# A float32 decoder trunk on one core: one activation table for the roots, memory turns inside the last values' projection, late weights turned a pass apart

## The reference

```python
mem_n = rmsnorm(mem, mem_norm_g)
y = rmsnorm(x, mix_norm_g) @ w_in              # q, k, v, gates of three head groups
fo = rmsnorm(forgetting_attention(q, k, v, log_f))   # 8 heads of 64
ho = rmsnorm(hgrn2_recurrence(hq, hf, hi)) * silu(hg) # 4 heads of 64
co = silu(channel_group_norm(causal_depthwise_conv(cu * sigmoid(cg), conv_w)))
x = x + concat([fo, ho, co]) @ w_out
# cross attention: q from x, k and v from the memory
k, v = split(mem_n @ w_xkv)
x = x + softmax(q @ k.T / 16) @ v @ w_xo
# mixture of 16 gated experts, top 1 group of 4, top 2 experts in it
x = x + sum_over_chosen(combine * (silu(t @ w_gate) * (t @ w_up)) @ w_down)
return rmsnorm(x, final_norm_g)
```

## Time and profile before

| What | us |
|---|---|
| median of 3 runs | 714.07 (713.83 to 714.19) |
| the profiled execution, its own time | 712.32 |
| its span | 710.3 |
| TensorE busy | 681.3 (96%) |
| VectorE busy | 280.6 (40%) |
| ScalarE busy | 153.2 (22%) |
| GpSimd busy | 78.5 (11%) |
| weight loads of TensorE | 331.4 (47%) |

### The profile page before, as it was taken

One profiled execution on the slowest core, in us unless ns is written; L12 is line 12 of the kernel. 1 busy time (PEld: TensorE's weight loads), 2 busy tenths in 40 slices (PEclk: granted clock), 3 DMA queues, 4 the chain that ended last, 5 costly groups with the idle time before them and its releaser, 6 DMA issues.

```text
span 710.3 us, 8420 instructions
## 1 busy us (share of the span) xinstructions
PE 681.3 (96%) x3398; PEld 331.4 (47%) x3398; DVE 280.6 (40%) x669; ACT 153.2 (22%) x315; POOL 78.5 (11%) x106
## 2 busy tenths in 40 slices
PE   7999999999999999999999999999999999999993
PEld 4644445453547665444444446545565333333331
DVE  3107599927034665213220006513334821212156
ACT  3011351003273444211000104301211010101112
POOL 3000081402020000000000000000001011110062
PEclk9999999999999999999999999999999999999998
DMA  8803240303036513300019406030029999999763
GB/s 288 308 0 119 82 154 1 119 1 108 15 119 180 178 60 119 118 1 0 1 36 395 161 0 237 0 119 30 30 87 341 363 372 389 376 375 392 268 219 137
DMA packets 69939, 111.90 MB, mean 158 GB/s; under 512 B 5648, under 2 KB 43780, under 8 KB 69900
## 3 DMA queue, kind: packets, MB, share of 16 engines
q1 hardware_dynamic: 65724, 96.16, 39.1%
q0 software_dynamic: 4176, 15.21, 5.8%
HBM read 101.90 MB, written 9.46 MB: 157 GB/s over the span
## 4 chain that ended last, share of the span: by engine, by line
PE 87%; DMA 4%; DVE 3%; ACT 3%; issue 1%; POOL 1%; SPq 0%; DVEq 0%; POOLq 0%; ACTq 0%
PE bank L1917 26%; PE bank L2193 16%; PE bank L1792 11%; PE bank L1927 6%; PE bank L1821 5%; PE bank L2263 2%; PE bank L1963 2%; PE bank L2243 2%; PE bank L2146 2%; PE bank L1949 2%; DMA W<-y_dram,A 2%; PE bank L1774 1%; PE bank L2124 1%; PE bank L2133 1%; PE bank L2035 1%; DMA x_sb<-in_x_dram 1%
## 5 line engine op out<-in xcount | busy, mean ns | idle before, releaser
L1917 PE MATMUL bank<-hT,W 128*128 128x512 f32 x368 | 159.7, 593 | 0.9 <-DVE hT L1071 0.9
L2193 PE MATMUL bank<-W,n_sb 128*128 128x512 f32 x256 | 114.2, 596 | 0.7 <-ACT n_sb L1039 0.7
L1917 PEld LDWEIGHTS bank<-hT,W 128*128 128x128 f32 x368 | 69.4, 190 | 87.5 <-issue 86.0
L1792 PE MATMUL bank<-W,A 128*32 128x512 f32 x672 | 84.8, 594 | 1.5 <-DVE A L1162 1.5
L2193 PEld LDWEIGHTS bank<-W,n_sb 128*128 128x128 f32 x256 | 47.1, 190 | 53.9 <-issue 52.3
L1425 DVE SCALAR_TENSOR_TENSOR A<-A,pc 128x511 f32<-128x511 f32 (+29 forms) x60 | 51.6, 860 | 2.0
L695 POOL TENSOR_TENSOR rstd<-ss,mhalf 128x1 f32<-128x1 f32 x14 | 7.7, 550 | 367.6 <-DVE ss L1055 203.1
L1792 PEld LDWEIGHTS bank<-W,A 128*32 128x32 f32 x672 | 23.1, 110 | 49.6 <-issue 47.6
L1821 PE MATMUL bank<-Dn,A 128*32 128x512 f32 x264 | 36.3, 595 | 0.0
L906 ACT ACTIVATE A<-bank 128x512 f32<-128x512 f32 (+1 forms) x22 | 12.1, 556 | 103.7 <-PE bank L1917 77.0
L1277 DVE TENSOR_TENSOR A<-A,bank 128x256 f32<-128x256 f32 x12 | 5.1, 421 | 71.7 <-ACT A L825 71.7
(11 more groups left out here) (306 smaller groups left out, 818.5 us busy)
## 6 DMA issues: line engine op xcount, KB each, us to landing
W<-in_w_gate_dram SPq DMA_DIRECT2D x14, 1024.0 KB, 13.3
W<-in_w_up_dram SPq DMA_DIRECT2D x14, 1024.0 KB, 14.5
Dn<-in_w_down_dram SPq DMA_DIRECT2D x11, 1024.0 KB, 13.8
W<-in_w_in_dram SPq DMA_DIRECT2D x5, 2048.0 KB, 9.3
W<-in_w_xkv_dram SPq DMA_DIRECT2D x4, 2048.0 KB, 8.3
hT<-in_w_down_dram SPq DMA_DIRECT2D x5, 1024.0 KB, 12.7
y_dram<-A POOLq DMA_DIRECT2D x10, 512.0 KB, 7.1
W<-in_w_out_dram SPq DMA_DIRECT2D x2, 2048.0 KB, 8.0
```

The source lines that it names most:

```text
L1792: mm = nc.tensor.matmul(PS[2 + b][r, :], xgT[:, b, c, r], gu_at[GU_HOME[e]][:, c, :], start=c == 0, stop=c == DC - 1)
L1917: mm = nc.tensor.matmul(bank[0:w, 0:n], lhs, src[:, c, 0:n], start=c == 0, stop=c == DC - 1)
L2193: mm = nc.tensor.matmul(PS[k % 4][:, :], src[:, c, t * P:(t + 1) * P], W[:, (n_load + n) % SLOTS, c, :], start=first and j == 0, stop=last ...
```

## The change

Three edits. On ScalarE, the table with Ln and Exp is asked for ahead of the convolution's roots. On TensorE, the last values' group (26) is written out as `last_values`, and the two halves of the memory's tile 1 are turned ahead of its chunks 4 and 6; on VectorE the two copies of tile 0 stand ahead of the heads' scalings, those of tile 1 behind. In the experts, the two late turns stand at the ends of passes 2 and 4 and their copies in passes 3 and 5.

```diff
--- before.py
+++ after.py
@@ -944,6 +944,7 @@
             ho_evac(0)
             proj_evac(22, 23)
             act.wait_ge(consts, 2)
+            nc.scalar.preload_act_table_set("natural_log_exp_and_others")
             for c in range(2):
                 act.wait_ge(cvar, c + 1)
                 inv_root(c, PS[4 + c][:, :], croot[c], crs)
@@ -1293,8 +1294,8 @@
                     y_half(p - 1)
                 if p == 1:
                     late_rows()
-                if 3 <= p < 3 + LATE:
-                    late_turned(p - 3)
+                if p in (3, 5):
+                    late_turned(p // 2 - 1)
 
             def add_row(k, t, w):
                 dve.wait_ge(fin_in[t][k], 16)
@@ -1529,6 +1530,8 @@
 
             for t in range(MT):
                 normed(dve, 1, t, mem_sb, mem_sb)
+            for k in range(2):
+                turn_evac(dve, 1, 0, k, PS[6 + k], memT, R_MEM)
             for p in range(HP):
                 dve.wait_ge(ho_rs, p + 1)
                 nc.vector.scalar_tensor_tensor(out=hob[p], in0=hob[p], scalar=pc[:, R_HG + p:R_HG + p + 1],
@@ -1536,8 +1539,8 @@
                 dve.wait_ge(ho_step, 2 * p + 1)
                 nc.vector.tensor_tensor(catT[:, 4 + p], hob[p], hgT[:, p], ALU.mult).then_inc(ho_step, 1)
 
-            for k in range(2 * MT):
-                turn_evac(dve, 1, k // 2, k % 2, PS[6 + k % 2], memT, R_MEM)
+            for k in range(2):
+                turn_evac(dve, 1, 1, k, PS[6 + k], memT, R_MEM)
 
 
             def f_scores(u, a):
@@ -1860,8 +1863,8 @@
 
                     pe.wait_ge(ht_sb, p)
                 turn_hidden(p % 2, ht_ps)
-                if 2 <= p < 2 + LATE:
-                    turn_late(p - 2)
+                if p in (2, 4):
+                    turn_late(p // 2 - 1)
             down_pass(NP - 1)
 
             pe.wait_ge(over_done, 1)
@@ -2108,10 +2111,16 @@
             pe.wait_ge(ho_sb, HP)
             for k in range(2):
                 turn_group(pe, 1, 0, k, PS[6 + k], mem_sb)
-            g = run([along(1, 3, 0, FW)], g, 5)
-            for k in range(2):
-                pe.wait_ge(turn_sb, TURN0[1] + k + 1)
-                turn_group(pe, 1, 1, k, PS[6 + k], mem_sb)
+            def last_values(bank):
+                for c in range(DC):
+                    if c in (4, 6):
+                        k = c // 2 - 2
+                        pe.wait_ge(turn_sb, TURN0[1] + k + 1)
+                        turn_group(pe, 1, 1, k, PS[6 + k], mem_sb)
+                    mm = nc.tensor.matmul(bank[:, 0:FW], hT[:, c, 3 * P:4 * P], W[:, 1, c, 0:FW], start=c == 0, stop=c == DC - 1)
+                return mm
+
+            g = run([last_values], g, 5)
 
 
             def qk(u):
```

## The result

The changed kernel took 708.40 us, the median of 5 executions (707.64 to 710.46). The kernel before, run beside it on the same chip, took 713.83 (5 executions, 712.83 to 714.19).

What follows compares the result with a forecast made beforehand. TensorE was taken as the bound (87% of the chain), so time is won where it stands still. Memory's gap 2.75 + late weights 1.05 = 3.8 us, subtracted from the median 714.07, gave 710.3 us, range 709.5 to 711.6.

Steps and rivals of the forecast that it cites:

- The memory's gap: Before the memory's first key projection on TensorE: it starts at 211.85 in place of 214.60, a gain of 2.75 us.
- The rival in which the table doesn't shorten the roots: ScalarE's roots stay slow: 1.35 + 1.05 = 2.4 us gained, 711.7 us in all; chance 0.06.
- The fallback of 1.35: Memory's gap if the roots stay slow: key projection at 213.25, so 1.35 us gained instead of 2.75.
- The four loads at the convolution's roots: Four of ScalarE's removed table loads, at the convolution: priced at nothing, covered by the values projections on TensorE.
- The mask of the second pair: VectorE's mask reading the second pair's decay sums: 4.0 us of room, 3.63 taken, 0.4 left; priced at nothing.
- The late weights: Turns of late tables in the expert passes: 1.31 us gained on TensorE, 1.05 counted after a wait at pass 10.
- pass 10 waits about 0.2: With TensorE 1.31 us earlier, pass 10 waits about 0.2 for up weights that had a margin of 1.11.
- bounds from 0 to 1.31: Late edit's gain: 1.31 us if the weights slip in, 0 if they are as late as they are now needed.
- The rule that was weighed: Expert passes: earlier stores on shared DMA engines take 0.3 us from the weights; late edit 0.75, sum 3.5.
- The tail: After pass 9's store: leaving 1 us earlier, it still finds room among the transfers; nothing counted.
- the 1.75 between profile and median: Median of three runs, 714.07, lies 1.75 us above the profiled 712.32; the trace can't tell where it arises.
- a rival 0.22: Pass 10 already waits for weights in unprofiled runs; late edit keeps 0 to 0.4: 2.95 us, 711.1; chance 0.22.

Runs made afterwards that it cites:

- e2_turns: The kernel before with tile 1 turned within the last values and the copies reordered, tables as before: 711.38 us, ratio 0.9973.
- e1_tables: The kernel before with the one table load ahead of the convolution's roots and nothing else: 711.09 us, ratio 0.9969.
- e10_after: The changed kernel unaltered, run a third time against the kernel before: 708.99 us, ratio 0.9937.
- e4_after: The changed kernel unaltered, run a second time against the kernel before: 709.14 us, ratio 0.9944.
- e7_light_before: The kernel before with ten experts' down matrices loaded by half their columns, 5 MB less: 712.93 us, ratio 0.9998.
- e8_light_after: The changed kernel with ten experts' down matrices loaded by half their columns, 5 MB less: 708.88 us, ratio 0.9942 to the kernel before.

## Why the prediction was right or wrong

**The memory's gap: right, to the hundredth.** Forecast 2.75, measured 2.75. The steps hold too. The roots end at 204.48 + 0.63 = 205.1 (205.2 forecast). The tile-0 copies run from 203.82 to 205.1 (203.7 to 205.0). The scalings are done by about 207.9 (208.0), and the key projection starts at 211.80 (211.85). The rival in which the table doesn't shorten the roots is out: Ln to Exp is 0.7 everywhere. The fallback of 1.35 for turns without tables came out at 1.45 in e2_turns. The tables by themselves give 1.45 as well (e1_tables), and the two overlap in 0.15, which neither the diff nor the busy times show; only working the chain out for all three cases does.

**The four loads at the convolution's roots: nothing,** as priced. In e1_tables and e2_turns, with and without them, the mean squares start at 201.22 and 202.17, and that order is the start's: from the end of the first load of x in the chain (3.16 + 8.03 and 3.40 + 8.72) to the mean squares it is 190.03 and 190.05.

**The mask of the second pair: covered, as argued.** Its decay sums were left 0.4 of room. In the changed kernel VectorE stands still for them, and then still waits for TensorE:

```profile
228.15 1.29 DVE L1593 TENSOR_TENSOR Dn<-Dn,causal 128x256 f32<-128x256 f32 x2 [0.66 <-DMA Dn<-lf_dram]
...
229.81 0.69 DVE L1557 CUSTOM_DVE_ANT_0 hT<-bank,A 128x512 f32<-128x512 f32 x1 [0.37 <-PE bank L2133]
```

The transfer is a wait of 0.66 on VectorE, and the scores behind it wait 0.37 more for TensorE. The room that is left is that 0.37, close to the forecast 0.4.

**The late weights: the gain right, the wait mis-sized.** TensorE saves 1.32 (1.31 forecast). The term "pass 10 waits about 0.2" measured 0.93, 0.54 and 0.12. That term was a difference of two small numbers: a margin of 1.11, read once, less 1.31. The landing of those weights, counted from the start of pass 0, was 118.02 before and between 117.74 and 118.68 in the other profiles with the full loads in their old order (that of e10_after has no landing). Without the late edit the four landings lie within 0.18 (117.84 to 118.02), so the reading of before was repeatable. With it they reach from 117.74 to 118.68, nearly the whole margin, and within the changed kernel alone the waits differ by 0.8. What had no row was how the landing moves once TensorE asks earlier; the prediction kept it where it was. The sum allowed for bounds from 0 to 1.31 there, and the edit's 0.39 to 1.20 lie within them. This term made the kernel slower than forecast, so it is not why the time fell below the range.

**The rule that was weighed.** The Trainium skill (DMA: Bandwidth & Descriptors, section "Issuing engines are not separate DMA queues") says that DMAs of all issuing engines run on the same 16 engines and interleave. From that the prediction worked out, with rows of this case, that the earlier stores would take 0.3 from the weights. The late edit alone had its weights 0.3 earlier than before (117.74 against 118.02), the whole change 0.7 and 0.3 later (118.68, 118.35). An effect of 0.3 is within that spread, and these runs don't settle it.

**The tail: nothing counted, 0.8 found, and it isn't the change's.** In the first pair of profiles the gathers took 0.33 less, and what follows the last addition took 15.61 in place of 16.10. In e4_after and e10_after these are 16.14 and 16.13, and the gathers 22.98 and 23.03. So that 0.8 belongs to one execution and not to the change, and it happened to make up for the wait at pass 10 of 0.93. That the profiles' 4.00 lies near the 3.8 is in part luck. The whole pair then reads: start 0.05, gap 2.75, middle 0.06, passes 0.39, pass 10 to the store -0.07, gathers 0.33, end 0.49: 4.00.

**The step that failed: from the sum to the median.** The prediction subtracted the sum from 714.07, the median of three executions, and gave the range "half a us to each side for the runs' own spread". But 62 executions of before have a median of 713.35 and reach from 711.24 to 715.97; three of them within 0.36 of each other said nothing of that. And the changed kernel's own executions spread from 707.64 to 710.57. With 713.35 in place of 714.07 the same sum gives 709.6; what then remains to the 709.0 of 17 executions is 0.6, a term of the same size as the interval of the difference. The same range around it, 708.8 to 710.9, would still have missed the 708.40: the median of those five executions lies 0.45 below that of the 17. The other base that the prediction had, the profiled 712.32, led to its 708.5, which is 0.1 from the result. That is luck as well: it was one execution, 1.0 below the median of the 62.

The forecast also guessed at the 1.75 between profile and median: "if they are waits for weights, the late edit is worth less there", and gave a rival 0.22 for it. e7_light_before leaves at most 0.9 of them to waits for the experts' weights, and its profile shows none. Where profiled executions differ outside the edits, it is at the start (201.22 to 202.80 at the mean squares) and in the gathers (22.48 to 23.98), which none of the edits touches.

One thing goes along with the time of the unprofiled executions and was not followed further: the mean granted clock. Of the kernel before, the 13 executions with 0.996 have a mean of 712.4, the 18 with 0.991 or 0.993 one of 714.5, and the profiled execution of 712.32 is one with 0.996. The profile of before shows where its clock is below 1.00 (windows: length, busy time of PE, PEld, DVE, ACT, POOL, clock, DMA share, GB/s):

```profile
698.00:700.00 2.00, 1.30 (x4) 0.23 (x2) 1.99 (x5) 1.75 (x3) 1.06 (x2) 1.00 0.00 0
702.00:704.00 2.00, 0.00 (x0) 0.00 (x0) 2.00 (x2) 0.99 (x2) 2.00 (x1) 1.00 0.43 172
704.00:706.00 2.00, 0.00 (x0) 0.00 (x0) 1.62 (x4) 0.72 (x1) 1.12 (x2) 0.67 0.60 244
706.00:708.00 2.00, 0.00 (x0) 0.00 (x0) 0.33 (x1) 0.00 (x0) 0.00 (x0) 0.50 0.62 252
```

It falls to 0.50 (1.2 GHz) only when TensorE has finished its last product, at 699.3, and so it is in all twelve profiles. There TensorE's clock costs nothing, and a longer idle end alone would lower the mean. Whether it falls earlier in the slower unprofiled executions, while TensorE still works, is not on record. So the lower clock may be a mark of a longer end or a part of the cause.

**What stays open.** Against the 713.4 of before, the means of the single edits are 2.3 (tables), 1.9 (turns) and 1.8 us (late) lower, where the traces show 1.45, 1.45 and 1.32; all three lie above, by 0.5 to 0.9 with a half width of about 0.6. So do the means of both memory edits together (3.4 against 2.8) and of the changed kernel with its down loads reordered (4.8 against 4.1). With light loads the two kernels lie 4.1 apart by their means, with a half width of 0.7, which is what the traces say (4.15). I have no mechanism for the excess, and no run here separates it from how the executions of before happened to fall.

## What to carry to other kernels

When a wait passes through several engines, work out the chain for each half of a fix as well as for the whole: here the tables and the reordering each gave 1.45 alone and 2.75 together. A margin against a full DMA stream, read before a change, doesn't hold to tenths once the change moves the requests: the landing lay within 0.18 us before the edit and within 0.94 with it, so the margin should enter as a range. Compare profiles stretch by stretch from a common event, and take the base for an absolute forecast from many executions: three that agree closely can all lie on one side.

## What the runs showed of the hardware that was not expected

- A matmul accumulation could be broken open for transposes into other banks at the bare cost of the transposes: 4 of them moved the chain by 0.44 (207.65 to 208.09), half of the 0.87 that 8 take between groups (203.34).
- The time of the same program reaches from 711.2 to 716.0 us over 62 executions, the slower ones with a lower mean granted clock (0.991 to 0.996). Part of the spread between profiles arises in the first microseconds: the first load of x that the chain passes through was issued at 3.16 to 3.79 and took 8.03 to 9.12 us.
- A 1 MB load issued by SyncE under a full stream held its queue for 6.29 us in one place and 0.80 in the same place with lighter loads (the up matrix issued at 636.20 in the changed kernel, and at 638.03 in e8_light_after). So a table of issue times from one kernel can't be shifted to another with a different load on the queue. That the bytes still outstanding set the hold is my reading of these two; only the lighter loads were tried.
